# Gate and up products of two feed-forward blocks by seven half-size products per slot, in place of eight

## The reference, cut to what matters

```python
def swiglu_ffn(h, w_gu, w_down):
    g, u = jnp.split(h @ w_gu, 2, axis=-1)
    return (jax.nn.silu(g) * u) @ w_down

for i in range(DEPTH):                       # DEPTH = 2
    x = x + 0.5 * swiglu_ffn(rmsnorm(x, n_ffn1[i]), ffn1_w_gu[i], ffn1_w_down[i])
    x = x + mixer(rmsnorm(x, n_mix[i]))      # gated linear attention, then pooling
    x = x + mem_cross_attn(rmsnorm(x, n_xattn[i]), rmsnorm(mem, n_mem[i]), ...)
    x = x + 0.5 * swiglu_ffn(rmsnorm(x, n_ffn2[i]), ffn2_w_gu[i], ffn2_w_down[i])
return rmsnorm(x, n_final)
```

## Time and profile before

| | |
|---|---|
| median of three executions | 1993.26 us |
| the profiled execution: span | 1992.3 us |
| PE (matmul) busy | 1983.5 us, 9182 matmuls |
| DVE busy | 930.9 us (47%) |
| ACT busy | 710.2 us (36%) |
| POOL busy | 160.8 us (8%) |
| mean DMA rate | 108 GB/s |

### The profile page before, as it was taken

The page is one execution under the profiler, slowest core; times in us unless marked ns, Lnnn a source line. Parts: engine busy times, 40 slices in busy tenths (PEclk is TensorE's granted clock), DMA queues, the critical chain, the costliest instruction groups (busy, mean ns, idle before and its releaser), DMA issues.

```text
span 1992.3 us, 23096 instructions
## 1 busy us (share of the span) xinstructions
PE 1983.5 (100%) x9182; PEld 1654.4 (83%) x9182; DVE 930.9 (47%) x1007; ACT 710.2 (36%) x865; POOL 160.8 (8%) x201
## 2 busy tenths in 40 slices
PE   9999999999999999999999999999999999999998
PEld 7888888888898888888888888888898888888887
DVE  5343443487865654434343443433287544434323
ACT  5222232256554543222222322222156443322222
POOL 2000001100112120000001000000112022200000
PEclk9999999999999999999999999999999999999999
DMA  5323352323434533232223323222353324432221
GB/s 176 105 88 102 100 142 76 104 64 106 129 126 127 169 106 106 84 105 88 96 95 100 106 84 105 87 98 95 121 165 114 103 85 127 158 105 96 94 95 74
DMA packets 204153, 214.53 MB, mean 108 GB/s; under 512 B 21970, under 2 KB 186960, under 8 KB 204096
## 3 DMA queue, kind: packets, MB, share of 16 engines
q1 hardware_dynamic: 180416, 192.95, 29.6%
q0 software_dynamic: 6432, 17.64, 3.4%
q10 hardware_dynamic: 17248, 3.16, 0.9%
HBM read 203.23 MB, written 10.49 MB: 107 GB/s over the span
## 4 chain that ended last, share of the span: by engine, by line
PE 96%; DVE 1%; DMA 1%; ACT 1%; issue 1%; SPq 0%; ACTq 0%; POOL 0%; DVEq 0%
PE ps L368 32%; PE ps L369 32%; PE ps L370 32%; DMA p_scratch<-sq 0%; ACT w_hi L1198 0%; DVE w_lo L1731 0%; DMA raw<-in_ffn_w_gu 0%; DVE sums L2213 0%; DMA p_tok<-p_scratch 0%; DVE sums L2233 0%; SPq L390 0%; DVE up L2411 0%; SPq L418 0%; PE ps L943 0%; PE ps L1138 0%
## 5 line engine op out<-in xcount | busy, mean ns | idle before, releaser
L368 PE MATMUL ps<-h_hi,w_hi 128*128 128x512 f32 (+1 forms) x1728 | 667.3, 386 | 0.2 <-DVE h_lo L1734 0.2
L369 PE MATMUL ps<-h_lo,w_hi 128*128 128x512 f32 (+1 forms) x1728 | 665.8, 385 | 0.0
L370 PE MATMUL ps<-h_hi,w_lo 128*128 128x512 f32 (+1 forms) x1728 | 665.8, 385 | 0.0
L1731 DVE TENSOR_TENSOR w_lo<-raw,w_hi 128x2048 fp32r<-128x2048 f32 (+4 forms) x195 | 417.4, 2141 | 461.8 <-ACT w_hi L1198 461.8
L1198 ACT ACTIVATE w_hi<-raw 128x2048 fp32r<-128x2048 f32 (+4 forms) x195 | 347.6, 1783 | 271.0 <-PE ps L370 266.9
L368 PEld LDWEIGHTS ps<-h_hi,w_hi 128*128 128x128 f32 x1728 | 324.7, 188 | 65.8 <-DVE h_lo L1734 0.9
L370 PEld LDWEIGHTS ps<-h_hi,w_lo 128*128 128x128 f32 x1728 | 324.6, 188 | 64.8
L369 PEld LDWEIGHTS ps<-h_lo,w_hi 128*128 128x128 f32 x1728 | 324.7, 188 | 64.0
L368 PE MATMUL ps<-mid_hi,w_hi 128*128 128x512 f32 x528 | 205.6, 389 | 0.0
L370 PE MATMUL ps<-mid_hi,w_lo 128*128 128x512 f32 x528 | 205.5, 389 | 0.0
L369 PE MATMUL ps<-mid_lo,w_hi 128*128 128x512 f32 x528 | 205.5, 389 | 0.0
(11 more groups left out here) (361 smaller groups left out, 1909.2 us busy)
## 6 DMA issues: line engine op xcount, KB each, us to landing
raw<-in_ffn_w_gu SPq DMA_DIRECT2D x87, 1024.0 KB, 5.1
raw<-in_ffn_w_down SPq DMA_DIRECT2D x34, 1024.0 KB, 4.9
raw<-in_x_w_kv SPq DMA_DIRECT2D x16, 1024.0 KB, 5.9
raw<-in_gla_w_in SPq DMA_DIRECT2D x12, 1024.0 KB, 5.1
raw<-in_ffn_w_down SPq DMA_DIRECT2D x12, 768.0 KB, 4.3
raw<-in_x_w_q SPq DMA_DIRECT2D x8, 1024.0 KB, 4.9
raw<-in_x_w_o SPq DMA_DIRECT2D x8, 1024.0 KB, 6.1
raw<-in_gla_w_out SPq DMA_DIRECT2D x8, 512.0 KB, 3.5
```

The lines of the kernel that those rows point to most:

```text
L368: nc.tensor.matmul(out_ap, left[0], right[0], start=first, stop=False)
L369: nc.tensor.matmul(out_ap, left[0], right[1], start=False, stop=False)
L370: return nc.tensor.matmul(out_ap, left[1], right[0], start=False, stop=last)
L1731: return nc.vector.tensor_tensor(out_ap, value, hi.bitcast(F32), ALU.subtract)
```

## The change

**What is computed.** In blocks 1 and 2 a slot now holds 128 gate and the 128 matching up columns. All but the first two slots of a block (20 of 22) are computed as a 2 x 2 block product in the form of Strassen and Winograd: the 1024 inner rows are halved, the tokens are halved (`TH` = 256), and gate and up are the two output rows. Seven products P1 to P7 take the place of eight. Each is 4 row chunks (`KH`) x 3 = 12 matmuls of 128x256, so a slot has 84 of them.

**Sums ahead.** Four sums of activations are made once per block (`sum_x`, `x_sums`, split into `s_hi` and `s_lo`): ACT scales a chunk (`scale_x`), DVE makes four sums of 256 columns, ACT and DVE split them. This is done for 4 chunk pairs in `feed_last_pairs`, between the residuals and feeds of the last four chunks of the stage ahead. Four sums of weights per slot (`w_sums`) are made by DVE, or by POOL for a run's first slot (`weight_sums`). Each of the seven weight forms of a slot is split apart (`form_hi` on ACT, `form_lo` on DVE, 128x512 each).

**Sums behind.** P1 and P2 add up in bank 6, P5 stands in bank 7, P6 adds onto a copy of P1 that ACT has put into a third bank (SEEDED), DVE adds P5 and puts the sum into the bank for P3 (U4_SEEDED), P7 and P4 add onto the third bank. P4 of a slot is taken by PE in the next slot, behind P6.

**The order in the block.** The block is cut in two parts of 11 inner chunks: gate/up slots 0 to 10 (two plain, nine mixed), then a down product over 11 chunks that is added to `x`, then slots 11 to 21 (eleven mixed) and the down product over the other 11. A down pair has slots of 6 and 5 chunks. The number of down matmuls stays 528. A run of mixed slots ends with `last_block` (the last P4), then `half_down`. The weights of a slot are loaded by two DMAs of 512 KB in rows of 512 bytes, before one of 1 MB in rows of 1 KB.

The diff, cut to its core:

```diff
+    def place_mixed(n):
+        for part in range(2):
+            for s in range(part * HALF, (part + 1) * HALF):
+                if s < PLAIN_FIRST:
+                    place(("gu", n, s), 2, 2, C, loads=2)
+                else:
+                    ...
+                    place(("gu", n, s), 0, 0, C, mixed=True, loads=2)
+            for pair in range(C // 2):
+                for g, (_, rows) in enumerate(HALF_GROUPS):
+                    place(("down", n, part, pair, g), 2, 2 if g == 1 else 0, rows)
...
+            def weight_sums(n, part):          # on POOL
+                pool.wait_ge(raw_loaded[w % 2], loaded[w])
+                nc.gpsimd.tensor_tensor(w_sums[:, 0:2], *outer_columns(w), ALU.subtract).then_inc(sig.w_sum_ready, 1)
+                nc.gpsimd.tensor_tensor(w_sums[:, 2], quarter(w, 1, 1), w_sums[:, 0], ALU.subtract)
+                nc.gpsimd.tensor_tensor(w_sums[:, 3], quarter(w, 1, 0), w_sums[:, 2], ALU.subtract)
...
+            def mixed_slot(n, part, l, j=None):   # on PE
+                form_ready(P1)
+                block_product(n, m, P1, 6)
+                form_ready(P5)
+                block_product(n, m, P5, 7)
+                form_ready(P6)
+                pe.wait_ge(sig.mixed_act_step, count(3, act_step(m, SEEDED)))
+                block_product(n, m, P6, b)
+                if l > 0:
+                    form_ready(P4)
+                    pe.wait_ge(sig.mixed_dve_step, count(6, dve_step(m - 1, C22_READY)))
+                    block_product(n, m, P4, before)
+                form_ready(P2)
+                block_product(n, m, P2, 6)
+                form_ready(P7)
+                pe.wait_ge(sig.mixed_dve_step, count(6, dve_step(m, U4_SEEDED)))
+                block_product(n, m, P7, b)
+                pe.wait_ge(sig.w_lo_ready, count(1, mixed_slots[m] + 1))
+                block_product(n, m, P3, d)
...
+            def feed_last_pairs(f, pair, split_after, residual):   # on DVE
+                if pair == 2:
+                    for m in (4, 5):
+                        residual(m)
+                        feed(f, m)
+                    sum_x(f, 0)
+                    split_next(split_after)
+                    x_sums_lo(f, 0)
+                    sum_x(f, 1)
+                else:
+                    residual(6)
+                    feed(f, 6)
+                    x_sums_lo(f, 1)
+                    residual(7)
+                    feed(f, 7)
+                    sum_x(f, 2)
+                    split_next(split_after)
+                    x_sums_lo(f, 2)
+                    sum_x(f, 3)
+                    sums_lo(f)
+                    x_sums_lo(f, 3)
```

More of the change, by code:

```diff
@@ L773, in tile_products @@
                     bank = chunk_bank(o) if g == 0 else o % 4
-                    s = at[("down", 3, half, g)].slot % 2
+                    s = area[at[("down", 3, half, g)].slot]
                     hi, lo = wide(w_hi[:, s]), wide(w_lo[:, s])
@@ L875, in first_spread, with activation_form, block_product @@
                 spread_rms(0)
+            def activation_form(i, kk):
+                low, high = slice(0, TH), slice(TH, SEQ)
+                if i in X_SUM_OF:
+                    return s_hi[:, X_SUM_OF[i], kk, :], s_lo[:, X_SUM_OF[i], kk, :]
+                k, ts = {P1: (kk, low), P2: (kk + KH, low), P4: (kk + KH, high)}[i]
+                return h_hi[:, k, ts], h_lo[:, k, ts]
+            def block_product(n, m, i, bank):
+                w = mixed_slots[min(m, len(mixed_slots) - 1)] if i != P4 else mixed_slots[m - 1]
+                hi, lo = form(w_hi, w, i), form(w_lo, w, i)
+                for kk in range(KH):
+                    right_hi, right_lo = activation_form(i, kk)
+                    to, fresh = ps[:, bank, 0:TH], i in (P1, P5) and kk == 0
+                    nc.tensor.matmul(to, hi[:, kk, :], right_hi, start=fresh, stop=False, skip_group_check=True)
+                    nc.tensor.matmul(to, hi[:, kk, :], right_lo, start=False, stop=False, skip_group_check=True)
+                    last = nc.tensor.matmul(to, lo[:, kk, :], right_hi, start=False, stop=kk == KH - 1,
+                                            skip_group_check=True)
+                last.then_inc(sig.product_done, 1)
@@ L877, in ffn @@
             def ffn(n, between=None):
                 hh = (h_hi, h_lo)
+                if n in MIXED:
+                    project(("gu", n, 0), hh, feed=(None, 3, 4, 7)[n])
+                    project(("gu", n, 1), hh)
+                    for part in range(2):
+                        mixed_slot(n, part, 0)
+                        with pe.Fori(0, (mixed_count(n, part) - 1) // 2) as j:
+                            for l in (1, 2):
+                                mixed_slot(n, part, l, j)
+                        last_block(n, part)
+                        half_down(n, part)
+                    return
@@ new lines, in mixed_ffn @@
+            def mixed_ffn(n, between):
+                norm_root((None, 3, 4, 7)[n])
+                load_silu()
+                for part in range(2):
+                    mixed_run(n, part)
+                    if part == 1 and between is not None:
+                        between()
+                    if (n, part) == (2, 1):
+                        band_split()
+                    f = FEED_AFTER[n]
+                    for pair in range(C // 2):
+                        split_next(at["down", n, part, pair, 0].slot)
+                        w = at["down", n, part, pair, 1].slot
+                        if part == 1 and n + 1 in MIXED and pair >= 2:
+                            feed_last_pairs(f, pair, w)
+                        elif part == 1:
+                            feed(f, 2 * pair)
+                            feed(f, 2 * pair + 1)
+                            split_next(w)
+                        elif pair < 3:
+                            split_next(w)
@@ L1442, in memory @@
                 else:
[L1443 removed]
+                    act.wait_ge(sig.product_done, OPENED + PRODUCTS * mixed_end(2, 1))
                 for c in range(C):
@@ L1586, in cross @@
                 for pair in range(4):
+                    if i == 0 and pair >= 2:
+                        feed_last_pairs(3, pair, at[("xo", 0, pair)].slot)
+                        continue
                     for m in (2 * pair, 2 * pair + 1):
```

517 lines of the change are left out of this document (484 added, 33 removed).

## The result

The changed kernel takes 1997.24 us, the median of 14 executions (1994.98 to 1998.12), against 1993.32 for the kernel before beside it (1992.94 to 1994.41). The ratio is 1.0018, with a 95% interval of 1.001 to 1.0025: slower by some 3.9 us, where 2.5 us faster was forecast. The profiled span is 1995.6 us, 3.3 more than the 1992.3 of before.

The account below looks back on a forecast made before the run. The prediction took PE to bound the kernel, busy 1983.5 of 1992.3 us. -32.1 + (12.7 + 11.1) + 2 x 0.5 + 4 x 1.2 = -2.5 us gave 1990.8 us; 8-in-10 range 1977 to 2009.

Parts of the forecast that it names:

- Part 1: PE in mixed slots: 10.08 us for a plain slot's 10.88, a gain of 32.1 us over both blocks.
- Part 2: DVE in a steady mixed slot: 9.8 us of 10.08 taken, so PE sets the pace and the cost is 0.
- The cover of 0.3 us: Steady mixed slot: the time DVE has to spare before PE waits, 0.3 us a slot.
- the wait that I counted: Every steady mixed slot: DVE's half_lo of the slot before waits for ACT's high part, 0.5 us.
- DVE's pace: Rival: in steady slots DVE's instructions and hand-overs set the pace, 1999 to 2012 us; chance 0.22.
- waits between products: Rival: each of 280 product boundaries costs a restart of 0.11 us, 31 us in all, 2022 us; chance 0.06.
- Part 3: Way into blocks 1 and 2: PE stops cost 12.7 us into block 1 and 11.1 into block 2.
- The norm stop: Ahead of the norm matmuls in blocks 1 and 2: PE waits 7.7 us for DVE's acc_parts.
- POOL hides: Rival: POOL's adds fall into DVE's gaps or share; norm wait 2.4 us, time 1980.2 us; chance 0.24.
- the wait for P6: First mixed slot: PE waits 2.7 us for ACT's seed, and in block 1 another 1.2.
- The rival: Clock falls in the 7.7 us stop, 50 matmuls behind at 1.2 GHz; up to 8 us a block, 2007; chance 0.08.
- Part 4: Other edges: starts of a second part 0.5 us, twice; run ends 1.0 plus restarts 0.2, four times; loads 0.

Follow-up runs that it names:

- the experiment with three sums: Three extra DVE sums of 256 columns (0.99 us) in each of the 32 inner mixed slots of the changed kernel; 2010.94 us.
- the norm's sum first: Changed kernel with the low part of the norm's sum (acc_parts) made ahead of the last s_hi/s_lo and last four activation sums; 1997.71 us.
- work for PE: Changed kernel with 28 thrown-away matmuls before the norm of blocks 1 and 2: 2002.28 us with the second slot's weights, 1997.3 us with the slot just done's.
- The experiment: Changed kernel with ACT's and DVE's band split moved behind the split of pair 1's down weights in block 2's second part; 1992.7 us.
- POOL's edit: Changed kernel with POOL's weight sums for the first mixed slot of blocks 1 and 2 waiting until ACT has taken the norm's root; 1988.33 us.
- the early seeds: ACT's seed for P6 and DVE's for P3 made earlier in a block's first mixed slot, on top of the kernel with both edits; 1990.81 us.
- both edits: Changed kernel with POOL's weight sums behind the root and the norm's sum first; 1991.44 us.
- all together: Changed kernel with POOL's sums behind the root, acc_parts first, early seeds, later band split, down slots of 5 and 6 rows, inv_count moved; 1985.56 us.

## Why the prediction was wrong

**Part 1, PE's gain**: right, 0.120 us a matmul and 32.1 us.

**Part 2, DVE in the steady slot**: right that it costs nothing and right in the place that is nearest to failing. The cover of 0.3 us was too small: 0.42 in a slot, by the experiment with three sums. That the added sums fall partly into the wait that I counted would explain it; no run shows it. The two rivals on the steady slot, DVE's pace and waits between products, are refuted.

**Part 3, into a block**: 12.7 and 11.1 forecast, 12.0 and 11.1 measured. The norm stop (7.7 for 7.5 and 6.6) and its cause are right, and what the lock is worth nearly so: without POOL's weight sums beside DVE's the kernel is 8.9 us faster, for the 10.6 that *POOL hides* put on it with POOL's adds counted too. The 11.1 of block 2 stood there without its terms, so only the total can be compared. One thing is right only in sum. I had the clock full, with 8% for its fall, and it fell; the wait for P6 was 1.0 and not 3.9. That the sum still holds is not luck: the chain on DVE and ACT sets when P6 starts, so what PE loses ahead of P6 its wait there gives back, as the experiments with the norm's sum first and with work for PE show. The rival had priced just this cover, but took all 50 matmuls at half clock where 13 were, and 0.213 us more for each where 0.20 was measured.

**Part 4, the other edges**: this is the step that failed. I costed the starts and ends of runs and stopped there. The sentence "The gain of part 1 is spent at eight edges" holds for ACT's and DVE's lists only if nothing else stands in them, and at one of the four run ends something does: `memory(1)` and `band_split`. They stood there before too, at no cost: the list of rows showed no stop, and I took this as a price of zero for a place whose cover the change takes away. ACT, then DVE, in order of time in the kernel before, at the same place:

```profile
1344.81 0.45 ACT L1198 ACTIVATE later_hi<-band 128x288 fp32r<-128x288 f32 x1 [7.37 <-POOL band L526]
...
1346.20 1.47 ACT L1198 ACTIVATE w_hi<-raw 128x1536 fp32r<-128x1536 f32 x1
...
1347.71 1.76 DVE L1731 TENSOR_TENSOR w_lo<-raw,w_hi 128x1536 fp32r<-128x1536 f32 x1 [1.89 <-ACT w_hi L1198]
```

The split behind the bands was that of the third down slot, and the down product had begun at 1330.7: two slots of 8 rows, 96 matmuls or 21.8 us, lay ahead of the third, until 1352.5. In the halved block two slots of 6 and 5 rows, 66 matmuls or 15.0 us, lie ahead of the slot behind the bands. Before, `w_lo` was over at 1349.5, 18.8 us into the down product, and PE wanted it at 21.8: 3.0 us to spare. Now it is over at 1407.1, 17.8 us into a down product that began at 1389.3, and PE wants it at 15.1: 2.7 us late. The experiment gives this 4.5 us, the stop of 2.8 and the half clock behind it, which is two thirds of the miss of 6.4. The rest: run ends 1.1 (1.48 in place of 1.2 each; with both splits shorter by 0.51 together each end lost 0.5 less, so they are what PE waits for), an edge of 0.6 at the cross attention's keys that I didn't look into, less 0.7 in block 1, and 0.3 of the span that no stop on my list accounts for; and the median stands 1.6 us above the profiled span where I took 1.0.

The range held the time. 1997.24 lies at the edge of 1997.2 that the prediction drew between same and slower. Slower had a chance of 0.32, nearly all of it for other mechanisms: DVE's pace, the clock and waits between products. What it was is a forgotten neighbour in an in-order list.

What stays open: the 0.6 us at the cross attention's keys, and how low the way into a block can go. By the starts on PE it was 6.9 us at the least (block 2 with POOL's edit), and 7.8 or more in block 1 in every version that left PE's own work as it was.

## What to carry to other kernels

When a change shortens a stage or cuts its slots smaller, go through every engine's list over the whole stage and list all foreign work that stands in it, above all instructions that wait for a third engine; what the old length hid needs its cover worked out anew. A stop in front of a chain that ends later costs nothing, so find the last link before moving an early one: the norm's sum first, the work for PE during the stop and the early seeds each shortened PE's longest wait and moved the time by 0.6 us at most, while taking POOL out of DVE's way, which changed no order, gave 8.9 us. And keep POOL's two-tensor work away from DVE's work on two tensors in SBUF where DVE is the one that PE waits for.

## What the runs showed of the hardware

**The clock falls in short stops, and not in all of them.** Stops on PE and the granted clock right behind them:

| stop | kernel and place | clock behind it |
|---|---|---|
| 7.5, 6.6 | changed kernel, norm | half |
| 5.5 | both edits, P6 | half |
| 3.4 | POOL's edit, norm of block 1 | half |
| 3.3 | POOL's edit, norm of block 2 | full |
| 2.8 | changed kernel, pair 1 | half |
| 2.8 | norm's sum first, pair 1 | full |
| 2.4 | all together, P6 | full |
| 2.4 | all together, block 2, P1 of the second mixed slot | half |

The rows for 3.4 and 3.3 us, in the kernel with POOL's edit, then those for the two of 2.4 us, in the first kernel with all edits together:

```profile
745.00:750.60 5.60, 5.49 (x13) 4.36 (x14) 5.01 (x9) 3.91 (x5) 2.92 (x2) 0.50 0.31 84
...
1100.30:1105.00 4.70, 4.70 (x21) 3.87 (x22) 3.58 (x2) 3.77 (x5) 2.25 (x1) 1.00 0.29 73
...
760.10:762.90 2.80, 2.76 (x23) 2.79 (x24) 1.89 (x3) 1.36 (x3) 0.00 (x0) 1.00 0.00 0
...
1123.80:1127.10 3.30, 3.29 (x15) 3.29 (x16) 1.91 (x4) 1.25 (x4) 0.00 (x0) 0.50 0.00 0
```

Stops of 2.4 us went either way within one kernel, so did 3.4 and 3.3, and 2.8 at one place in two kernels. The length alone doesn't tell. I had priced a stop at its length. The half clock behind it took up to 2.7 us more of PE's time: nothing in the end where a later wait hid it (the norm), 1.6 at pair 1, 1.4 at P6 with both edits.

**The lock of POOL and DVE goes by what an instruction reads.** DVE's sum of 256 columns with both inputs in SBUF took 3.36 us beside POOL and 0.42 without. Its reciprocal over one tensor took 3.29 with POOL beside it and 3.29 to 3.35 elsewhere. The kind of operation is not what decides: a TENSOR_TENSOR like that sum, with one input in PSUM, doesn't wait either. DVE, then POOL, in an earlier stage of the changed kernel:

```profile
588.09 0.69 DVE L2521 TENSOR_TENSOR x<-ps,x 128x512 f32<-128x512 f32 x1 [0.26 <-PE ps L429]
...
587.65 1.34 POOL L678 TENSOR_TENSOR acc<-acc,sq 128x512 f32<-128x512 f32 x1 [0.81 <-ACT sq L1617]
```

Both are as long as alone (0.68 and 1.33 to 1.34). In that trace 11 DVE instructions with one input in PSUM start while a POOL sum runs, and all last 0.68 to 0.69 us; those with both inputs in SBUF are longer by about what is left of POOL's.
